# The middle expert packs of TensorE as one loop, and the last pack read by k-slices and by columns

## The reference

```
hf = rms_norm(x)                                  # 256 x 1024
for e in range(32):
    a   = silu(hf @ w_gate[e]) * (hf @ w_up[e])   # 1024 -> 512
    out = out + combine[:, e:e+1] * (a @ w_down[e])   # 512 -> 1024
out = rms_norm(x + out)
```

## Time and profile before

| | us |
|---|---|
| median of 3 runs (lowest, highest) | 706.2 (706.0, 706.61) |
| profiled execution | 705.62 |
| its span, first to last instruction | 703.8 |
| PE busy in the span | 539.7 |
| DMA, mean over the span | 344 GB/s |

### The profile page before, as it was taken

How to read it: one execution, slowest core, us unless ns; L and a number is a source line. 1 busy time by engine, 2 the same in 40 slices (tenths; PEclk the granted TensorE clock), 3 DMA queues, 4 the chain that set the end, 5 groups by cost and what they waited for, 6 DMA issues and landing times.

```text
span 703.8 us, 7579 instructions
## 1 busy us (share of the span) xinstructions
PE 539.7 (77%) x3247; PEld 328.8 (47%) x3247; DVE 205.4 (29%) x451; ACT 65.9 (9%) x134; POOL 43.5 (6%) x73
## 2 busy tenths in 40 slices
PE   8999999999999999898684482494667448247765
PEld 7888888888878565352141140141123114012411
DVE  4888896969513133010000010010000001000002
ACT  3010000001111022100010000000000000000102
POOL 6001211111200021000000000000000000000000
PEclk9999999999999999999797797788679679678989
DMA  8960903364179858999999999999999999999993
GB/s 339 424 295 0 357 3 120 119 250 163 66 303 426 337 219 317 408 429 427 432 428 432 428 429 428 430 431 425 430 430 431 427 431 431 428 426 430 428 428 160
DMA packets 18901, 241.93 MB, mean 344 GB/s; under 512 B 2353, under 2 KB 2481, under 8 KB 4402
## 3 DMA queue, kind: packets, MB, share of 16 engines
q1 hardware_dynamic: 18432, 239.83, 81.7%
q10 hardware_dynamic: 434, 1.58, 0.6%
HBM read 240.35 MB, written 1.05 MB: 343 GB/s over the span
## 4 chain that ended last, share of the span: by engine, by line
PE 50%; DMA 46%; SPq 1%; DVE 1%; ACT 1%; issue 1%; POOL 0%; DVEq 0%; PEldq 0%; ACTq 0%
DMA x_region<-in_w_down 39%; PE bank L1183 28%; PE bank L1462 8%; DMA x_region<-in_last_halves 6%; PE bank L1319 4%; PE bank L1195 2%; PE bank L1507 2%; PE bank L1172 1%; PE bank L1529 1%; SPq L478 1%; DMA ring<-in_mix 1%; PE bank L1287 1%; PE bank L1418 1%; PE bank L1297 1%; PE bank L1343 0%
## 5 line engine op out<-in xcount | busy, mean ns | idle before, releaser
L1454 PE MATMUL bank<-ring,work_region 128*32 128x512 f32 x560 | 112.2, 668 | 68.7 <-DMA early_region<-in_w_up 68.3
L1183 PE MATMUL bank<-x_region,ring 128*128 128x256 f32 x640 | 141.0, 381 | 1.7 <-ACT ring L643 1.1
L1183 PEld LDWEIGHTS bank<-x_region,ring 128*128 128x128 f32 x640 | 120.8, 190 | 21.3 <-ACT ring L643 2.8
L1462 PE MATMUL bank<-ring,work_region 128*32 128x512 f32 x288 | 55.7, 745 | 49.6 <-DMA x_region<-in_w_down 49.6
L1454 PEld LDWEIGHTS bank<-ring,work_region 128*32 128x32 f32 x560 | 29.5, 121 | 112.5 <-issue 112.5
L1107 DVE TENSOR_TENSOR work_region<-work_region,bank 128x512 f32<-128x512 f32 x8 | 8.2, 1028 | 200.5 <-PE bank L1454 190.9
L1454 PE MATMUL bank<-rot_region,work_region 128*32 128x512 f32 x112 | 50.9, 609 | 13.2 <-DMA ring<-in_w_gate 10.8
L1454 PE MATMUL bank<-early_region,work_region 128*32 128x512 f32 x112 | 60.9, 706 | 0.0
L1183 PE MATMUL bank<-early_region,ring 128*128 128x256 f32 x256 | 56.0, 380 | 1.4 <-ACT early_region L648 1.4
L1462 PE MATMUL bank<-x_region,work_region 128*32 128x512 f32 x96 | 55.6, 745 | 0.0
L1462 PEld LDWEIGHTS bank<-ring,work_region 128*32 128x32 f32 x288 | 15.0, 134 | 86.0 <-issue 86.0
(11 more groups left out here) (243 smaller groups left out, 514.8 us busy)
## 6 DMA issues: line engine op xcount, KB each, us to landing
ring<-in_w_up SPq DMA_DIRECT2D x21, 2048.0 KB, 38.8
ring<-in_w_down SPq DMA_DIRECT2D x18, 2048.0 KB, 38.8
ring<-in_mix SPq DMA_DIRECT2D x16, 2048.0 KB, 10.3
ring<-in_w_gate SPq DMA_DIRECT2D x14, 2048.0 KB, 45.6
ring<-in_first SPq DMA_DIRECT2D x8, 2048.0 KB, 15.5
rot_region<-in_w_gate SPq DMA_DIRECT2D x7, 2048.0 KB, 35.3
s_region<-in_w_gate SPq DMA_DIRECT2D x7, 2048.0 KB, 39.8
early_region<-in_w_up SPq DMA_DIRECT2D x7, 2048.0 KB, 48.1
```

The lines of the kernel that those rows point to most:

```text
L1183: ins = MM(dst, w[:, k, n * P:(n + 1) * P], rhs[:, k, :], start=k == 0, stop=k == kn - 1)
L1454: ins = MM(bank[to][quarter(e), :], xT[:, k, quarter(e)], of_expert[e][:, FF * k:FF * k + FF], start=k == 0, stop=k == KD - 1)
L1462: ins = MM(bank[6 + h][quarter(e), :], actT[:, c, quarter(e)], of_expert[e][:, D * c + 512 * h:D * c + 512 * h + 512], start=c == 0, stop= ...
```

## The change

```diff
+LAST_COLUMNS = ((6, 0, 512), (7, 512, 256), (5, 768, 256))      # bank, first column, columns
+LAST_DOWN = ((0, 0, 2), (0, 2, KF), (1, 0, KF), (2, 0, KF - 1), (2, KF - 1, KF))  # part, k-slices
...
-            for pk in range(1, PACKS - 1):
-                whole_pack(0, pk + 1, expert_units, main_loaded(pk))
-                if pk == 1:
-                    spread_gain()
+            with pe.Fori(1, PACKS - 1) as pk:
+                whole_pack(0, pk + 1, expert_units, loaded_in_turn(pk))
+            spread_gain()
             pe.wait_ge(most_ready, 1)
             most_r = pe.value_load(most[0:1, 0:1], min_val=0, max_val=T)
             with pe.If(most_r > SLOTS):
                 over_experts()
                 pe.sem_inc(over_done, 1)
-            whole_pack(0, PACKS, expert_units, main_loaded(PACKS - 1), with_down=False)
+            last_gate_up()
             last_down()
```

```diff
+            def last_gate_up():
+                first = units_before(PACKS - 1)
+                tokens_in(0, PACKS)
+                rest_of_tokens(0, PACKS)
+                ...
+                for w in range(8):
+                    wt = expert_view(expert_loaded(first + w), 1024)
+                    for kk in range(2):
+                        k = 2 * (w // 2) + kk
+                        for e in range(PACK):
+                            ins = MM(bank[4 + w % 2][quarter(e), :], xT[:, k, quarter(e)], wt[:, e, FF * kk:FF * kk + FF], ...)
+                    if w < 6:
+                        ins.then_inc(expert_units, 1)
+                    else:
+                        ins.then_inc(up_psum[0], 1)
+                        pe.wait_ge(up_psum[0], 2 * PACKS - 7 + w)
+                        pe.sem_inc(expert_units, 1)
+                    if w in (5, 6):
+                        keep_clock(7, 12)
+                turn_act(0, PACKS)
             def last_down():
+                for i, (part, c0, c1) in enumerate(LAST_DOWN):
+                    ...                      # wait for transfer i, then 4 matmuls for each k-slice c0 to c1
+                    if i == 0:
+                        keep_clock(4, 9)
+                    if i == 1:
+                        pe.wait_ge(y_act[0], PACKS)
+                        add_to_tokens(0)
+                    if i == 2:
+                        pe.wait_ge(y_dve[0], PACKS)
+                        add_to_tokens(1)
+                pe.wait_ge(fg_ready, 2 * TB)
+                pe.wait_ge(y_dve[0], PACKS + 1)
+                add_to_tokens(2)
```

More of the change, by code:

```diff
@@ L38 @@
 ROUNDS = T // SLOTS
+LAST_COLUMNS = ((6, 0, 512), (7, 512, 256), (5, 768, 256))
+LAST_DOWN = ((0, 0, 2), (0, 2, KF), (1, 0, KF), (2, 0, KF - 1), (2, KF - 1, KF))
 def expert_units_in_order():
     units = [(0, "pair", w) for w in range(8)] + [(0, "rows", c) for c in range(KF)]
[L49 to L52, removed]
+    for pk in range(1, PACKS - 1):
+        units += [(pk, what, e) for what in ("gate", "up", "down") for e in range(PACK)]
     last = PACKS - 1
-    return units + [(last, "rows", c) for c in range(KF - 1)] + [(last, "half", h) for h in range(2)]
+    units += [(last, "pair", w) for w in range(8)]
+    return units + [(last, "columns", i) for i in range(len(LAST_DOWN))]
 UNITS = expert_units_in_order()
@@ L101, in mixer_schedule, with block_kernel @@
     return order + [("ypre", YB - 1), ("gelu", YB - 1)]
-def block_kernel(nc, x_in, x_columns, columns, mix, s5_b, s5_c, norm_ffn, route_w, route_b, first, last_rows, last_halves,
+def block_kernel(nc, x_in, x_columns, columns, mix, s5_b, s5_c, norm_ffn, route_w, route_b, first, last_pairs, last_left, last_third, last_most, last_least,
                  w_gate, w_up, w_down, norm_final, out):
@@ L455, in expert_source @@
                 if what == "pair":
-                    return first[part]
+                    return first[part] if pk == 0 else last_pairs[part]
                 if what == "rows":
-                    return first[8 + part] if pk == 0 else last_rows[part]
-                if what == "half":
-                    return last_halves[part]
+                    return first[8 + part]
+                if what == "columns":
+                    return (last_left[0], last_left[1], last_third, last_most, last_least)[part]
                 view = {"gate": gate_v, "up": up_v, "down": down_v}[what]
@@ L741, in _ @@
             expert_pack(0, PACKS, gate_used(PACKS - 1))
[L743 to L758, removed]
+            spent = slots[slot_of(units_before(PACKS - 1) + 1)][0]
+            junk = spent[:, 0:6 * 512].rearrange("p (i n) -> p i n", i=6)
+            for part, (_, at, n) in enumerate(LAST_COLUMNS):
+                for b in range(TB):
+                    i = TB * part + b
+                    act.wait_ge(moe_psum, i + 1)
+                    nc.scalar.activation(junk[:, i, 0:n], bank[2 * b + at // 512][:, at % 512:at % 512 + n], ACT.Square,
+                                         accum_out=stat[:, 6 + i:7 + i]).then_inc(sumsq, 1)
             for b in range(TB):
                 act.wait_ge(rstd, 4 + b)
+                act.wait_ge(fg_ready, b + 1)
                 nc.scalar.activation(o_sb[:, b, 0:512], o_sb[:, b, 0:512], ACT.Copy, scale=stat[:, 4 + b:5 + b]).then_inc(out_act, 1)
@@ L1087, in count_most, with expert_pack @@
                 V.tensor_copy(most[:], cnt_f[:]).then_inc(most_ready, 1)
-            def expert_pack(o, done, number, rank_of, weight_of, weighted=None):
+            def expert_pack(o, done, number, rank_of, weight_of, weighted=None, whole=True):
                 shape = [P, TB, PACK, SLOTS]
@@ L1152, in _, with keep_columns @@
[L1152 to L1158, removed]
+            def keep_columns(part):
+                from_bank, at, n = LAST_COLUMNS[part]
+                dve.wait_ge(down_psum[0], 2 * PACKS - 1 + part)
+                V.tensor_copy(y_sb[:, at:at + n], bank[from_bank][:, 0:n]).then_inc(y_dve[0], 1)
@@ new lines, in share @@
+            def share(part, b):
+                i = TB * part + b
+                to = stat[:, b:b + 1] if part < 2 else stat[:, 2 + b:3 + b]
+                dve.wait_ge(sumsq, LAST + 1 + i + 1)
+                if part:
+                    dve.wait_ge(left_ready, 3 + TB * (part - 1) + b + 1)
+                V.tensor_scalar(to, stat[:, 6 + i:7 + i], 1.0 / D, stat[:, b:b + 1] if part else EPS,
+                                ALU.mult, ALU.add).then_inc(left_ready if part < 2 else meansq, 1)
@@ new lines, in times_gain @@
+            def times_gain(part, b):
+                _, at, n = LAST_COLUMNS[part]
+                V.tensor_tensor(o_sb[:, b, at:at + n], bank[2 * b + at // 512][:, at % 512:at % 512 + n], g_fin[:, at:at + n],
+                                ALU.mult).then_inc(fg_ready, 1)
+            keep_columns(1)
+            for part in range(2):
+                for b in range(TB):
+                    share(part, b)
+                    times_gain(part, b)
+            keep_columns(2)
+            for b in range(TB):
+                share(2, b)
@@ L1468, in rest_of_tokens, with whole_pack @@
                 pe.wait_ge(wselT_ready[o], done)
-            def whole_pack(o, done, units, loaded_of, with_down=True):
+            def whole_pack(o, done, units, loaded_of):
                 tokens_in(o, done)
@@ L1481, in whole_pack @@
                 turn_act(o, done)
[L1482 to L1486, removed]
+                whole_down(o, done, loaded_of(2))
+                pe.wait_ge(down_psum[o], done * 2)
+                pe.sem_inc(units, PACK)
+                combine(o, done)
             def first_pack():
@@ L1559, in main_loaded, with add_to_tokens @@
-            def main_loaded(pk):
-                def of(i):
-                    first = units_before(pk) + PACK * i
-                    return [slots[expert_loaded(first + e)][0] for e in range(PACK)]
+            def add_to_tokens(part):
+                _, at, n = LAST_COLUMNS[part]
+                for b in range(TB):
+                    MM(bank[2 * b + at // 512][:, at % 512:at % 512 + n], wselT[:, b, :], y_sb[:, at:at + n],
+                       start=False, stop=True, skip_group_check=True).then_inc(moe_psum, 1)
@@ new lines, in last_down @@
+            def last_down():
+                first = units_before(PACKS - 1, ("pair",))
+                for i, (part, c0, c1) in enumerate(LAST_DOWN):
+                    to, _, n = LAST_COLUMNS[part]
+                    slot = slots[expert_loaded(first + i)][0]
+                    wt = slot[:, 0:(c1 - c0) * PACK * n].rearrange("p (c e n) -> p c e n", e=PACK, n=n)
+                    for c in range(c0, c1):
+                        for e in range(PACK):
+                            ins = MM(bank[to][quarter(e), 0:n], actT[:, c, quarter(e)], wt[:, c - c0, e, :],
+                                     start=c == 0, stop=c == KF - 1)
+                    if c1 == KF:
+                        ins.then_inc(down_psum[0], 1)
+                    if i == 0:
```

(21 more changed lines are left out.)

51 lines of the change are left out of this document (14 added, 37 removed).

## The result

| | before | after |
|---|---|---|
| median (lowest, highest), 4 runs each | 706.1 (705.28, 706.61) | 710.77 (709.76, 711.64) |
| profiled execution | 705.62 | 709.76 |
| its span | 703.8 | 707.9 |

The ratio is 1.0059, with a 95% interval of 1.0041 to 1.0077: the change makes the kernel slower, by 4.2 us on 706.1 (the medians themselves differ by 4.7). The forecast was 711.0.

A forecast was written before the change was run, and what follows sets the result against it. Weights' DMA bounds the kernel before; TensorE the new last pack. Gather 658.0, plus 6.5, 22.7, 13.5 and 7.8, gives span 708.5, 4.8 over 703.8; median 706.2 + 4.8 = 711.0. Likeliest case 708.4 to 712.2, all cases 703.4 to 712.6.

The forecast's parts named there:

- The jump: TensorE's jump over the unused routine before the last pack's gather: stalls 6.5 us uncovered, gather at 658.0 instead of 652.2.
- The spreading: Gain spread after pack 6, ahead of the jump: from combine at 644.06 until ACT is done at 650.5.
- Gather to first product: Last pack, from gather at 658.0 to first gate product at 664.5: 6.5 us, as before.
- Gate and up with fillers: Last pack's gate and up by k-slices, all TensorE: 22.7 us, so down matmuls start at 687.2.
- Down: Last pack's down by columns, nearly all bytes landed: 13.5 us, last down matmul ends at 700.7.
- The tail: From the end of the last down matmul to the span's end: 7.8 us, where it was 9.3.
- The loop at nothing: Loop over packs 1 to 6 with five jumps back: costs 0, even at 6.51 us each, hidden under waits.
- Landings: Arrival of the last pack's weights, 4.88 us a unit: third down transfer at 688.2, last at 693.0.
- Rival A: The forward jump does not stall, down matmuls wait for landings: span 701.5, median 703.9, 2.3 us less; chance 0.24.
- B: A cheaper jump (1 to 2.5 us) or shorter waits cancel out: within 0.2%; chance 0.05.
- C: Loop reaches the DMA queue, or the jump needs a second fetch: 713 to 715; chance 0.09 together with Rival D.
- Rival D: Last pack at lower granted clock: each us of array work costs 0.4 to 1 more; chance 0.09 with C.

The follow-up runs named there:

- e5: Changed kernel without TensorE's read of the count, its jump and the routine jumped over (test only): 701.45 us, 0.9936 of the kernel before.
- e1: Changed kernel with the gain spread after pack 1 again, pack 1 written out, loop over packs 2 to 6: 703.77 us, 0.9967 of the kernel before.
- e2: Changed kernel with packs 1 to 6 written out instead of the loop: 710.66 us, 1.0068 of the kernel before.
- e8: Changed kernel with two packs in the loop's body (three turns): 710.42 us, 1.0053 of the kernel before.
- e9: Changed kernel with three packs in the loop's body (two turns): 709.65 us, 1.0041 of the kernel before.
- e3: Changed kernel without the three groups of filler matmuls in the last pack: 702.37 us, 0.9932 of the kernel before.
- e7: Changed kernel with the gain spread behind the jump instead of ahead of it, ACT's copies too: 707.74 us, 1.0012 of the kernel before.
- e6: Kernel before with only the spreading of the gain moved to after pack 6: 705.52 us, 0.9989 of the kernel before.
- e4: Changed kernel with the gain spread early and no fillers in the last pack: 702.87 us, 0.9952 of the kernel before.
- e10: e1 with fillers only after the seventh unit and the first down transfer: 703.24 us, 0.9956 of the kernel before.

## Why the prediction was right

The forecast was 711.0, from a gather that starts late and a last pack bound by TensorE. Step by step:

- **The jump.** Forecast 6.5 us in full view; measured 5.85. The 7.44 us of idle TensorE ahead of the gather are this and the wait for ACT ahead of it. e5 takes it away and gains 8.7 us, e1 puts it back under the combine and gains 6.5.
- **The spreading.** Combine to ACT's end forecast 6.4 us; measured 641.43 to 647.65, 6.2.
- **Gather to first product** forecast 6.5, measured 7.07: 0.45 us of it is one more stop for "issue" inside the gather, at 660.19, and its first 8 records took 2.08 us, where they took 1.66; the mean granted clock was 0.50 from 648 to 657.
- **Gate and up with fillers** forecast 22.7, measured 661.53 to 684.28, 22.75.
- **Down** forecast 13.5, measured 684.28 to 700.08, 15.8. This is the term that was too small, by 2.3 us. Some 1.7 us of it: the first down group took 3.17 us and the fillers behind it 2.67, where e1 has 1.92 and 2.27, at a mean granted clock of 0.83 from 684 to 694. The other 0.6 is in the sum itself, since the traces without that drop show 14.2 (e1, e2); the terms I listed add up to 13.4, not 13.5. The array had stood still 1.2 and 0.7 us just ahead of it; in e2 the same pauses left the group at 1.92 us. Why the clock fell here and not there stays open.
- **The tail** forecast 7.8, measured 700.08 to 707.9, 7.8.
- **Where the sum was lucky.** From combine to end I had 64.5 us, and it was 66.5. But the profiled execution reached that combine at 641.43, not at 644.06. These 2.6 us early hid the 2.0 us that the sum was short, and the span came out at 707.9 for a forecast 708.5. In the other three kernels with the same last pack and the late spreading (e2, e8, e9) combine to end took 65.2, 64.1 and 65.5 us, nearer to the sum, and the combine started at 642.3 to 643.4. So the mechanism held, and that the span agrees within 0.6 us is in part luck. The start scattered from 641.4 to 644.2 over the profiled runs of this study (unrolled kernels 642.9 to 644.2, looped ones 641.4 to 643.6). Whether the loop has a part in it is not settled; e2's time says that it is small.
- **The loop at nothing** was right, as far as e2 can tell. The price that I named for it without cover, 5 x 6.51 us, was not: a jump back takes 0.21 us (median), so there was nothing to cover.
- **Landings.** I had the third down transfer at 688.2 and the last at 693.0, 4.8 us later. In e3 the third lands near 687.7 and the last 2 MB behind it within about 4 us (4 GB/s from 692 to 693); the end then hangs on the third: its matmuls, DVE's copy, two products, the next two groups, 5.6 us in all.

Rival A (no stall, 703.9) did not occur, and e5 shows what it would have been worth: without the jump the time is 0.9936 of before, 4.5 us less, where A had 2.3 less. A's reason, down groups that wait for their landings, is not what e5 shows: none of its down groups waits for DMA. Rivals B and C did not occur. Rival D (the lower clock in the last pack) occurred in part: the 1.7 us of the down groups in the profiled execution are of its kind.

On the jumps, the Trainium skill ("Runtime: NRT & Kernel Launch", section "Instruction fetch mechanics") gives the instruction memory two blocks of 16 KiB and a stop for every taken branch out of them. The forward jump bears it out (5.8 to 6.7 us in every kernel that has it). The jump back over four and six packets does not: 0.25 us at most, and no refetch. The same section also gives the memory of TensorE 128 KiB, and six packets of some 16 KB fit in that. Here code that had been run once was still there. That the forward jump waits for code is an inference, but the traces support it: in the kernel before, the changed one, e1, e2 and e7 one instruction packet moves while the jump is under way, 2 to 3 us before its end. In the changed kernel this is the window of 651.5 to 652.0, in a jump from 648.5 to 654.35:

```profile
q8 instruction: 1, 0.02, 13.7%
```

## What to carry to other kernels

Ask of every operation that is moved what its old place was hiding: four matmul records and a wait, without a cost in e6, cost 6.5 us here, since they pushed a jump of 5.9 us out of the shadow of the combine and the last pack had no slack left. Filler matmuls that keep the clock up can be free only while the engine is ahead of its data; once its start slips, each is added to the end (9.0 us for three groups here), so look whether the waits behind them still name a DMA, and time the kernel without them: where TensorE was ahead they gained nothing that these runs can tell. A stage that gives up its slack (here the old last pack's 7.8 us of waiting for up weights) must be checked against everything that had been living on it.

## What the hardware showed that I had not expected

- A jump forward over code never run: 5.84 to 6.73 us on TensorE; the jumps of SP, ACT and DVE over their own parts of that routine take 0.05 to 0.07 us. A jump back over the code of three packs, six packets of some 16 KB: 0.25 us at most, and no fetch.
- The same 16 records take 1.92 us or 3.2 to 3.6, and the wait just ahead of them doesn't settle which. In e4 groups behind waits of 2.29 and 2.75 us were slow, and in e10 one behind 1.35 us was not. But behind the 0.69 us ahead of the first down group, the changed kernel took 3.17 us and e1, e2 and e5 took 1.92.
- The end of a stream is not sharp. Single microseconds of the kernel before (busy times, granted clock, DMA share, GB/s):

```profile
689.00:690.00 1.00, 1.00 (x12) 0.13 (x4) 0.00 (x0) 0.00 (x0) 0.00 (x0) 1.00 0.64 270
...
692.00:693.00 1.00, 0.60 (x2) 0.30 (x2) 0.00 (x0) 0.35 (x1) 0.00 (x0) 1.00 0.08 33
```

The share of busy DMA engines falls over 4 us, from full before 689 to 8% in the last.
